# A decoder layer on one core: the SSD branch's causal mask put on pairs of tokens in the selector product, and each channel group's squares added on GpSimd

## The reference, cut to what matters

```python
def step(h, inp):                       # chunks of L = 128 tokens; a sample sequence is one of 8
    xc, dtc, bc, cc = inp
    cum = jnp.cumsum(dtc * A, axis=1)
    lmat = jnp.exp(jnp.where(mask, cum[:, :, None] - cum[:, None, :], -jnp.inf))
    xdt = xc * dtc[..., None]
    cb = jnp.einsum('btgn,bsgn->btsg', cc, bc)
    y = (jnp.einsum('btsg,btsge,bsgep->btgep', cb, lmat, xdt)
         + jnp.exp(cum)[..., None] * jnp.einsum('btgn,bgepn->btgep', cc, h))
    ...
gated = ys.reshape(Bsz, T, S_INNER) * jax.nn.silu(z.astype(f32))
gg = gated.reshape(Bsz, T, S_GROUPS, S_INNER // S_GROUPS)
gg = gg * lax.rsqrt(jnp.mean(gg * gg, axis=-1, keepdims=True) + EPS)
```

## Time and profile before

| | |
|---|---|
| median of 3 runs (lowest to highest) | 1386.93 us (1385.72 to 1388.42) |
| profiled execution, its own time | 1389.19 us |
| its span, from first to last instruction | 1387.5 us |
| busy in the span: PE, DVE, ACT, POOL | 1295.7, 761.8, 628.6, 176.6 us |
| mean granted TensorE clock, share of full | 0.973 |

### The profile page before, as it was taken

The page is one execution under the profiler, slowest core; times in us unless marked ns, Lnnn a source line. Parts: engine busy times, 40 slices in busy tenths (PEclk is TensorE's granted clock), DMA queues, the critical chain, the costliest instruction groups (busy, mean ns, idle before and its releaser), DMA issues. The chain is left out here.

```text
span 1387.5 us, 22794 instructions
## 1 busy us (share of the span) xinstructions
PE 1295.7 (93%) x9224; PEld 1176.4 (85%) x9224; DVE 761.8 (55%) x1317; ACT 628.6 (45%) x1093; POOL 176.6 (13%) x312
## 2 busy tenths in 40 slices
PE   6799999997999889899999999999999979999997
PEld 3699999995988667678998888888989969999997
DVE  1644454335875446755378675865365564555443
ACT  3433333324667435544355664554563343333433
POOL 3000000001540312110023222111100010000010
PEclk9899999998999999999999999999999989999998
DMA  9856666876343577883774445463335464444451
GB/s 302 232 184 198 221 204 205 228 205 215 121 122 107 194 269 269 277 271 119 203 204 130 120 135 172 124 206 114 113 95 152 152 202 133 152 152 133 136 145 51
DMA packets 258862, 241.57 MB, mean 174 GB/s; under 512 B 8607, under 2 KB 242479, under 8 KB 258710
## 3 DMA queue, kind: packets, MB, share of 16 engines
q1 hardware_dynamic: 249262, 211.03, 50.2%
q0 software_dynamic: 9024, 28.91, 6.0%
q10 hardware_dynamic: 472, 0.17, 0.1%
HBM read 209.88 MB, written 30.21 MB: 173 GB/s over the span
## 5 line engine op out<-in xcount | busy, mean ns | idle before, releaser
L2010 DVE TENSOR_TENSOR w_lo<-ring,w_hi 128x1024 fp32r<-128x1024 f32 (+1 forms) x264 | 336.3, 1275 | 447.4 <-ACT w_hi L1427 447.2
L1427 ACT ACTIVATE w_hi<-ring 128x1024 fp32r<-128x1024 f32 (+1 forms) x264 | 289.5, 1097 | 562.3 <-PE bank L730 557.1
L730 PE MATMUL bank<-u_hi,w_hi 128*128 128x320 f32 x1536 | 274.0, 322 | 22.4 <-ACT w_hi L1427 19.0
L730 PEld LDWEIGHTS bank<-u_hi,w_hi 128*128 128x128 f32 x1536 | 239.3, 195 | 37.2 <-issue 30.5
L730 PE MATMUL bank<-u_lo,w_hi 128*128 128x320 f32 x1536 | 260.0, 312 | 0.0
L730 PE MATMUL bank<-u_hi,w_lo 128*128 128x320 f32 x1536 | 256.5, 309 | 0.0
L730 PEld LDWEIGHTS bank<-u_lo,w_hi 128*128 128x128 f32 x1536 | 237.5, 191 | 0.0
L730 PEld LDWEIGHTS bank<-u_hi,w_lo 128*128 128x128 f32 x1536 | 233.7, 188 | 0.1
L598 POOL TENSOR_TENSOR arena<-arena 128x320 f32<-128x320 f32 x24 | 20.9, 873 | 634.5 <-ACT arena L1439 621.4
L727 PE MATMUL aux<-ident,arena 128*128 128x128 f32 (+6 forms) x404 | 62.3, 280 | 22.5 <-ACT arena L1413 9.5
L727 PEld LDWEIGHTS aux<-ident,arena 128*128 128x128 f32 (+6 forms) x404 | 45.3, 145 | 36.5 <-issue 17.3
(11 more groups left out here) (348 smaller groups left out, 1523.0 us busy)
## 6 DMA issues: line engine op xcount, KB each, us to landing
ring<-in_w_in SPq DMA_DIRECT2D x52, 1024.0 KB, 5.4
ring<-in_ff_w SPq DMA_DIRECT2D x44, 1024.0 KB, 5.5
ring<-in_ada_w SPq DMA_DIRECT2D x36, 1024.0 KB, 7.0
ring<-in_ff_w SPq DMA_DIRECT2D x32, 704.0 KB, 4.9
arena<-in_state_mlstm_C SPq DMA_DIRECT2D x32, 512.0 KB, 4.6
out_s_C<-arena POOLq DMA_DIRECT2D x32, 512.0 KB, 4.6
ring<-in_w_pa SPq DMA_DIRECT2D x8, 1024.0 KB, 7.8
arena<-in_state_ssm SPq DMA_DIRECT2D x32, 256.0 KB, 3.6
```

Source lines behind the costliest of these rows:

```text
L730: return nc.tensor.matmul(dst, lhs, rhs, start=first, stop=last)
L1427: nc.scalar.activation(w_hi[v.split_no % 2][:, 0:v.kc, :], panel_part(v), ACT.Copy).then_inc(S["hi_done"], 1)
L2010: V.tensor_tensor(w_lo[r][:, 0:v.kc, :], panel_part(v), w_hi[r][:, 0:v.kc, :].bitcast(FP32), ALU.subtract)\
```

## The change

Masking. The pairwise mask moves into the one selector product: rows 0 to 63 of `cum_rows`, zero before, now hold `pair_mask` (-1e30 where the query column lies before the whole *pair* of key tokens), and rows 0 to 63 of the selector map key partition p to row p/2. The selector is now a full 128x128 tile, one of three in turn; for each head POOL copies the head's column into its lower half (`picks`, 32 copies of 64x128 in all), and PE waits for it (`masks_ready`). What a pair mask leaves open is the one element above the diagonal in a pair; it is closed by zeros in the scores: DVE, not ACT, now takes them out of PSUM, two of the four blocks times a 0/1 triangle (`masked_scores`), and `weights` first limits the exponentials to 1.

Squares. POOL adds the four tiles of squares of a group (`sum_of_group`, one operation of 640 columns and one of 320), and PE's sum has 3 products in place of 12. The sum of group 1 moves one unit later.

Preparation. Seven small DVE operations go (two come) in the stage before, and one of 448 columns at the first `xbc` unit; POOL makes the tables instead.

```diff
+            def picks(gr, i):
+
+                for n in range(8 * gr + 2 * i, 8 * gr + 2 * i + 2):
+                    if n >= 3:
+                        pool.wait_ge(S["cb_bc"], n - 2)
+                    nc.gpsimd.tensor_copy(head_pick[n % 3][64:128, :], head_rows[:, n:n + 1].to_broadcast([64, 128])).then_inc(S["masks_ready"], 1)
+                pool.wait_ge(S["masks_ready"], MH + n + 1)
+
+            picks(0, 0)
             for gr in range(SG):
-                for u in phase_units(gr):
+                for i, u in enumerate(phase_units(gr)):
                     if u.name == "xbc":
                         conv_side(u, pad2, 3)
+                    if i < 4 and (gr, i) != (SG - 1, 3):
+                        picks(gr + (i + 1) // 4, (i + 1) % 4)
...
+            def sum_of_group(gr):
+
+                pool.wait_ge(S["gsq_ready"], gr + 1)
+                ch.link(nc.gpsimd.tensor_tensor(gsq[gr][:, 0:2, :], gsq[gr][:, 0:2, :], gsq[gr][:, 2:4, :], ALU.add))
+                nc.gpsimd.tensor_tensor(gsq[gr][:, 0, :], gsq[gr][:, 0, :], gsq[gr][:, 1, :], ALU.add).then_inc(S["sq_summed"], 1)
+
             for r in range(6):
                 send_tails(4 + r, r, out["p_sconv"], out["s_sconv"])
+                if r == 0:
+                    sum_of_group(0)
+                    sum_of_group(1)
+                if r == 1:
+                    sum_of_group(2)
+                if r == 4:
+                    sum_of_group(3)
...
-                    mm(x[:, 0:448], head_pick[:, n:n + 1].to_broadcast([128, 128]), cum_rows[:, :], True, False)
-                    mm(x[:, 0:128], ident_r, causal[:, 0:128], False, False)
-                    mm(x[:, 256:448], ident_r, causal[:, 0:192], False, True).then_inc(S["cb_bc"], 1)
+                    pe.wait_ge(S["masks_ready"], MH + n + 1)
+                    mm(x[:, 0:448], head_pick[n % 3], cum_rows[:, :]).then_inc(S["cb_bc"], 1)
...
-                pe.wait_ge(S["gsq_ready"], gr + 1)
+                pe.wait_ge(S["sq_summed"], 2 + gr + 1)
                 for blk in range(3):
                     n = 128 if blk < 2 else 64
-                    for j in range(4):
-                        ins = mm(aux[0][0:n, 4 * blk + gr:4 * blk + gr + 1], gsq[gr][:, j, blk * 128:blk * 128 + n], ones[:, 0:1], j == 0, j == 3)
+                    ins = mm(aux[0][0:n, 4 * blk + gr:4 * blk + gr + 1], gsq[gr][:, 0, blk * 128:blk * 128 + n], ones[:, 0:1])
...
-                if gr > 0:
-                    act.wait_ge(S["w_ready"], 4 * gr)
-                act.wait_ge(S["cb_mm"], gr + 1)
-                ch.inc(copy(cbm[:, 0:384], banks[3][:, 0:384]))
-                copy(cbm[0:64, 384:448], banks[3][0:64, 384:448]).then_inc(S["cb_read"], 1)
...
+            def masked_scores(gr):
+
+                dve.wait_ge(S["cb_mm"], gr + 1)
+                if gr > 0:
+                    dve.wait_ge(S["w_ready"], 4 * gr)
+                blocks = banks[3][:, 0:384].rearrange("p (c t) -> p c t", t=128)
+                ch.inc(V.tensor_tensor(cbm[:, 0:384].rearrange("p (c t) -> p c t", t=128)[:, 0::2, :], blocks[:, 0::2, :],
+                                       tri_m.unsqueeze(1).to_broadcast([128, 2, 128]), ALU.mult))
+                ch.inc(V.tensor_copy(cbm[:, 128:256], banks[3][:, 128:256]))
+                V.tensor_tensor(cbm[0:64, 384:448], banks[3][0:64, 384:448], tri_sm, ALU.mult).then_inc(S["cb_read"], 1)
...
-                ch.inc(V.tensor_tensor(w[:, :, 0:384], w[:, :, 0:384], c[:, :, 0:384].to_broadcast([128, 2, 384]), ALU.mult))
+                ch.inc(V.scalar_tensor_tensor(out=w[:, :, 0:384], in0=w[:, :, 0:384], scalar=1.0, in1=c[:, :, 0:384].to_broadcast([128, 2, 384]),
+                                              op0=ALU.min, op1=ALU.mult))
```

More of the change, by code:

```diff
@@ L234, in build @@
         h_dec = sb("h_dec", [128, 16 * (SB + 1)])
-        ident_r, causal, head_pick = w_rest[0][:, 0:128], w_rest[0][:, 128:320], w_rest[0][:, 320:352]
+        head_pick = [w_rest[0][:, 128 * r:128 * r + 128] for r in range(3)]
+        pair_mask, tri_m = w_rest[2][0:64, 0:192], w_rest[2][:, 256:384]
+        tri_sm, head_rows = w_rest[3][0:64, 320:384], w_rest[3][64:128, 320:352]
         bt = w_rest[1][:, 0:384].rearrange("p (c n) -> p c n", n=SN)
@@ L2580, in _ @@
                         group_rows(gr)
+                        masked_scores(gr)
                     if i == 1:
```

36 lines of the change are left out of this document (22 added, 14 removed).

## The result

| | before | changed |
|---|---|---|
| median (lowest to highest), runs | 1387.51 us (1383.38 to 1390.19), 6 | 1378.82 us (1373.56 to 1381.55), 6 |
| profiled execution, its own time | 1389.19 us | 1379.06 us |
| its span | 1387.5 us | 1377.3 us |
| busy in the span: PE, DVE, ACT, POOL | 1295.7, 761.8, 628.6, 176.6 us | 1280.8, 764.8, 625.9, 207.2 us |
| mean granted TensorE clock | 0.973 | 0.972 |

PE's busy time falls by 14.9 us, about the ceiling of 13.6 us. POOL has 31 us more to do.

What follows compares the result with a forecast made beforehand. PE has the most work, but DVE holds it in the first units of groups 0 to 2. Phases -2.0, sums -1.8, clock +0.8 make -3.0 us: 1386.2 against the profiled execution, 1384 as median; range 1380 to 1388.

Steps and rivals of the forecast that it cites:

- the ceiling of 13.6 us: PE's own saving at most: 6.4 us from mask products of 32 heads, 7.2 us from four groups' sums.
- I take -1.8: Tail, sums of groups 0 to 2: -1.8 us, with POOL and DVE colliding, counted without a half-speed spell.
- The clock: +0.8: Tail, sums: even odds that a half-speed spell costing 1.5 us stays, +0.8 us.
- Group 3's sum: nothing: Tail, sum of group 3: no gain, as PE waits behind it for ACT's gate.
- The phases: -2.0 forecast: Four group phases: -0.4, -0.1, -0.1 and -1.4, together -2.0 us of 6.4.
- nothing for head 0: First head of each group: no gain, as PE's second selector product waits for ACT's copy of B's rows.
- The price of `masked_scores`: DVE's unbroken run in a group's first units: three added operations cost 0.8 us, between 0.42 and 1.26.
- The limit in `weights`: DVE's weights operations: limiting adds 0.05 us to each of two, 0.1 us a unit.
- No collisions in the tail: Rival, chance 0.20: POOL and DVE don't collide, the sums give -4.1, total -6.1 us, 1380.8 us.
- DVE doesn't hold PE: Rival, chance 0.07, groups 0 to 2: four times 1.4 and 4.1 make -9.7 us, 1377.2 us.
- it comes to nothing: Rival, chance 0.30: full half-speed spell, collisions, costlier POOL copies; -0.8 down to 0, 1386.1 to 1387 us.
- slower: Rival, chance 0.08: POOL comes late with the selector in three groups; +2.7 us, 1389.6 us.

Runs made afterwards that it cites:

- fill_wait: The changed kernel with ten full-width PE products, into columns nobody reads, added ahead of the tail's first column sum; 1381.47 us, 0.9957 of the kernel before.
- squares_only: The kernel before with only POOL's sums of squares added, mask and selector as before; 1385.35 us, 0.9986 of the kernel before.
- long_sums: The changed kernel with each of the three products of a group's column sum issued four times; 1390.03 us, 1.0028 of the kernel before.
- masking_only: The changed kernel with squares and their sums as before, 12 PE products a group; 1386.02 us, 0.9998 of the kernel before.
- sum3_on_pe: The changed kernel with group 3's sum made by PE in 12 products, without POOL's additions for it; 1378.82 us, 0.9935 of the kernel before.
- fill_both: As fill_wait, with eighteen more such products ahead of group 3's column sum; 1382.04 us, 0.9958 of the kernel before.
- scores_on_act: The changed kernel with ACT copying the scores from PSUM, without the triangle and without masked_scores on DVE; 1381.61 us, 0.9962 of the kernel before.
- double_picks: The changed kernel with each of POOL's 32 selector copies made twice; 1377.46 us, 0.9924 of the kernel before.
- sums_later: The changed kernel with group 0's sum moved one unit later, beside those of groups 1 and 2; 1382.51 us, 0.9964 of the kernel before.

## Why the prediction was wrong

The sign was right and so were the mechanisms in the phases; what failed is how the term for the sums in the tail was put together, and with it the size. The 24 runs of the changed kernel average 1378.7 +- 0.6 us, the 149 runs of the kernel before that were timed beside them and the other experiments 1386.8 +- 0.2: a gain of 8.0 +- 0.7 us (standard errors), where 3.0 were forecast. From group 0 on the traces explain 6.5 of it (mean 640.2 of four before, 633.7 of three after): +1.2 in group 0, -2.3 in groups 1 to 3, -4.3 in the tail's four units, -1.1 behind.

**The sums, the term that failed.** "I take -1.8" and "The clock: +0.8" gave -1.0 for groups 0 to 2. Measured over the tail's four units: 24.7 us against 27.9, 27.9, 29.4 and 30.9, so -3.2 to -6.2, in the mean -4.3. PE's saving was 4.9 us and the wait for group 0's sum 1.52 (forecast 1.5), the collision was there as well. Two steps were wrong.

First, I let PE wait for the sum of group 2 *and* put a half-speed spell on top, though the two run side by side. In the changed kernel the slowed PE is through with group 1's sum some 13.1 us after the start of the tail (969.33, by ACT's `w_hi`), and POOL has finished group 2 at 13.1 us too (982.39): no wait is left. The forecast had POOL there at 12.4 without collisions and at 14.1 to 15.3 with two or three of them; here one collision lengthens POOL's chain, the others fall on DVE. (Three of 1.2 us would have given 991.3, not the forecast's 990.6.) Where the spell is absent, in fill_wait and squares_only, POOL is ready at 14.0 and 13.8 us and group 2's sums end 2.2 and 2.4 us earlier than before: near the -1.8. So the wait by itself was sized about rightly; adding the spell to it was the mistake.

Second, I took the clock from one trace of the kernel before, which had the shortest spell that it shows, 3.4 us; two others have 6.8 and 10.2. long_sums and masking_only have still more half-speed time around long stretches of one-column products (17.0 and 13.6 us). So in these four units the clock is not worth +0.8 us to the change but, against the mean of four traces, some -1. Over the whole kernel it is worth next to nothing: the second spell in group 0 takes back what the tail gives, and the runs' clocks give 77.1 +- 0.6 us at half speed before and 76.4 +- 1.2 after. That is also why the parts don't add: masking alone leaves the 48 records and has 84.9 us.

**Group 3's sum: nothing.** Confirmed by sum3_on_pe, at a wait of 2.85 us for POOL. But the rest behind the tail is 1.1 us shorter in the mean (384.5 to 383.4), not nothing: the spell behind the gates, with its 1.4 us, is absent from all traces of the changed kernel and from one of four before. That it is absent because PE now comes late to the gates is argued from the rows and not shown: in sum3_on_pe, where the wait is out, the spell stays away too, and in fill_both, where the gates' waits are back and no spell stands ahead of them, it also does (383.7 us).

**The phases: -2.0 forecast, -3.0 measured** where no spell disturbs group 0 (58.7 to 58.1, and groups 1 to 3 from 166.8 to 164.5; they are -0.37, -0.37 and -1.56 us). The ways were right: nothing for head 0 (its wait grows from 0.29 to 0.42 us), DVE holds PE, group 3 gives its 1.4 and more. The price of `masked_scores`, 0.8, was 0.84. The limit in `weights` was priced at 0.1 a unit and costs nothing. Its price came from a pair of operations that is not alike, as the dearer one reads PSUM (`aux` in the earlier trace rows). In the forecast's sum that is 0.2 of the 0.27 us by which groups 1 and 2 came out better: PE starts heads 2 and 3 15.57 us after the group's start, before 15.53, where 0.2 later was forecast. In the three traces of the changed kernel group 0, with its two spells, is *longer*, by up to 0.9 us against the traces before with one; this is the +1.2 in the 6.5. Whether the masking brings the second spell was not tested.

**The rivals.** "No collisions in the tail" had the nearest number for the sums (-4.1) for a wrong reason: there are collisions. "DVE doesn't hold PE" came nearest to the time (1377.2), by luck: the waits for DVE and scores_on_act speak against it, and groups 1 and 2 gave 0.37 us each, not 1.4. Neither "it comes to nothing" nor "slower" occurred. No wait for POOL's selector copies appears, as forecast, not even in double_picks.

**What stays open.** 1.5 +- 0.7 us of the mean gain lies outside the 6.5 us. Ahead of group 0 the code that runs is nearly the same and the starts scatter over 11 us, so chance can make it; and three traces are few. Why squares_only's runs gain less than its trace was not settled, nor where a spell begins: the traces show what stood ahead of each, not a rule.

## What to carry to other kernels

Before sizing a saving of a few us on TensorE, look at the granted clock around it in more than one trace of the same kernel: one-column products cost here 1.5 to 2 times their own time, the rest through the clock (long_sums). The granted clock of every run is a cheap second look: here it told a spell in one trace from a habit of the kernel. Don't add a wait and a half-speed spell that stand one behind the other on the same engine: each can be the other's cover, and taking one away (sums_later, fill_wait) gave a slower kernel. Test parts of a change together as well as apart: here the parts gave 0.3 and 1.9 us, and the whole 8.

## What the runs showed of the hardware

- The limit is free on VectorE: SCALAR_TENSOR_TENSOR with min and product over 768 columns takes 952 ns, the product alone 948 (means of 16). The 57 ns between the pair in the earlier trace rows is no measure of it, as one of the two reads PSUM.
- TensorE's clock fell to 1.2 GHz *within* 48 one-column records while the rows show PE busy throughout (3.40 of 3.40 us ahead of 977.10 in masking_only; 5.32 and 6.66 us for 48 records where 4.83 stood). The Trainium skill (page "TensorE: Matmul & The Clock Gate", Part 1) says that a hardware monitor sets the clock by how busy the engine has been. A busy row in the profile was no protection here, and the measurement decides.
- Ten full-width products in a wait of 1.52 us: no spell behind the first sum in all four traces that had them, where the six traces with the same masking and sums and the unfilled wait had one. squares_only had none behind unfilled waits of 1.41 and 2.43 us, while fill_wait had one behind its wait of 2.43, so a wait alone doesn't decide it.
- GpSimd's addition of 640 columns took 1.55 to 1.58 us alone and 2.55 beside VectorE, its addition of 320 columns 0.86 and 1.73; VectorE's product of 320 columns took 0.49 us alone and 1.85 beside GpSimd.
